# Weighted sums of cached values: four heads in four strips of output partitions, and two full transposes for eight small ones

## The reference

```python
def cross_attn(h, mem_k, mem_v, w_xq, w_xo):
    b, L, _ = h.shape
    q = (h @ w_xq).reshape(b, L, X_HEADS, X_HEAD_DIM)
    s = jnp.einsum('blhd,bmhd->bhlm', q.astype(jnp.float32), mem_k.astype(jnp.float32)) * (X_HEAD_DIM ** -0.5)
    pr = jax.nn.softmax(s, axis=-1)
    o = jnp.einsum('bhlm,bmhd->blhd', pr, mem_v.astype(jnp.float32)).reshape(b, L, D_MODEL)
    return o.astype(h.dtype) @ w_xo
...
hs, nc, ns, npool = layer(hs, state_conv[l], state_ssm[l], state_pool[l],
                          cache_mem_k[l], cache_mem_v[l], PAST_LEN, p)
```

## Time and profile before

| what | value |
|---|---|
| median of 3 runs | 1350.93 us (1350.61 to 1351.19) |
| span of the profiled execution | 1353.3 us, 2.4 us over that median; no other time is given for it |
| TensorE busy | 1289.4 us, 95% |
| VectorE busy | 743.5 us, 55% |
| ScalarE busy | 451.3 us, 33% |
| instructions | 23876 |

### The profile page before, as it was taken

How to read it: one execution, slowest core, us unless ns; L and a number is a source line. 1 busy time by engine, 2 the same in 40 slices (tenths; PEclk the granted TensorE clock), 3 DMA queues, 4 the chain that set the end, 5 groups by cost and what they waited for, 6 DMA issues and landing times.

```text
span 1353.3 us, 23876 instructions
## 1 busy us (share of the span) xinstructions
PE 1289.4 (95%) x9801; PEld 1193.5 (88%) x9801; DVE 743.5 (55%) x1484; ACT 451.3 (33%) x752; POOL 150.2 (11%) x176
## 2 busy tenths in 40 slices
PE   6999999999999898799999998899999999999996
PEld 5999988888888897689999997449999999999996
DVE  5777865656667877864344438323543443433433
ACT  4444432333332124532234323223431231322322
POOL 1000011000112957400001000001100000000000
PEclk7999989999998899999999999899999999999998
DMA  6422322222123666432233728511222222223211
GB/s 220 113 82 73 95 66 64 63 63 63 32 63 98 206 195 192 124 117 86 86 119 101 274 93 292 207 62 46 96 94 94 94 94 94 93 93 93 95 63 63
DMA packets 139214, 147.54 MB, mean 109 GB/s; under 512 B 4210, under 2 KB 132386, under 8 KB 138817
## 3 DMA queue, kind: packets, MB, share of 16 engines
q1 hardware_dynamic: 119124, 126.98, 29.3%
q10 hardware_dynamic: 18096, 8.62, 2.3%
q0 software_dynamic: 1904, 10.65, 2.2%
HBM read 130.21 MB, written 16.68 MB: 109 GB/s over the span
## 4 chain that ended last, share of the span: by engine, by line
PE 85%; DVE 8%; ACT 2%; DMA 2%; POOL 2%; issue 1%; SPq 0%; DVEq 0%; ACTq 0%
PE slot L371 67%; PE slot L1862 2%; PE aux L1624 2%; PE aux L1617 1%; PE slot L1773 1%; PE aux L1618 1%; DVE w_lo L356 1%; PE aux L1603 1%; DVE junk L1387 1%; ACT w_hi L349 1%; PE aux L1835 1%; PE slot L1853 1%; DVE sring L1199 1%; POOL win_sum L555 1%; DMA vr<-in_conv_b 1%
## 5 line engine op out<-in xcount | busy, mean ns | idle before, releaser
L356 DVE TENSOR_TENSOR w_lo<-w_raw,w_hi 128x1024 fp32r<-128x1024 f32 x186 | 234.2, 1259 | 360.9 <-ACT w_hi L349 360.8
L349 ACT ACTIVATE w_hi<-w_raw 128x1024 fp32r<-128x1024 f32 x186 | 197.0, 1059 | 571.9 <-PE slot L371 535.8
L371 PE MATMUL slot<-a_hi,w_hi 128*128 128x260 f32 x1408 | 300.8, 295 | 0.7 <-DVE a_lo L1428 0.7
L371 PE MATMUL slot<-a_hi,w_lo 128*128 128x260 f32 x1408 | 286.1, 285 | 0.0
L371 PE MATMUL slot<-a_lo,w_hi 128*128 128x260 f32 x1408 | 285.3, 285 | 0.0
L371 PEld LDWEIGHTS slot<-a_hi,w_hi 128*128 128x128 f32 x1408 | 221.5, 191 | 18.9 <-issue 15.4
L371 PEld LDWEIGHTS slot<-a_lo,w_hi 128*128 128x128 f32 x1408 | 219.9, 191 | 0.0
L371 PEld LDWEIGHTS slot<-a_hi,w_lo 128*128 128x128 f32 x1408 | 219.5, 191 | 0.0
L371 PE MATMUL slot<-b_hi,w_hi 128*128 128x260 f32 x640 | 129.0, 283 | 1.6 <-DVE gate_b L1258 1.6
L371 PE MATMUL slot<-c_hi,w_hi 128*128 128x260 f32 x640 | 129.4, 283 | 0.2 <-DVE c_lo L1340 0.2
L371 PE MATMUL slot<-b_hi,w_lo 128*128 128x260 f32 x640 | 129.0, 283 | 0.0
(11 more groups left out here) (385 smaller groups left out, 1582.4 us busy)
## 6 DMA issues: line engine op xcount, KB each, us to landing
w_raw<-in_w_in SPq DMA_DIRECT2D x32, 1024.0 KB, 5.7
w_raw<-in_w_up SPq DMA_DIRECT2D x16, 1024.0 KB, 5.3
w_raw<-in_w_down SPq DMA_DIRECT2D x16, 1024.0 KB, 5.0
sring<-in_state_ssm SPq DMA_DIRECT2D x16, 512.0 KB, 4.2
out_ssm_sample<-sring ACTq DMA_DIRECT2D x16, 512.0 KB, 3.6
w_raw<-in_w_ssd_proj SPq DMA_DIRECT2D x8, 1024.0 KB, 5.1
cache<-in_cache_mem_k SPq DMA_DIRECT2D x8, 1024.0 KB, 7.6
cache<-in_cache_mem_v SPq DMA_DIRECT2D x8, 1024.0 KB, 5.1
```

The source lines that it names most:

```text
L349: nc.scalar.activation(w_hi[:, t % 2], w_raw[:, t // 2 % 2, :, t % 2 * P:t % 2 * P + P], ACT.Copy).then_inc(hi_ready, 1)
L356: nc.vector.tensor_tensor(w_lo[:, t % 2], w_raw[:, t // 2 % 2, :, t % 2 * P:t % 2 * P + P], w_hi[:, t % 2].bitcast(F32), ALU.subtract).the ...
L371: last = nc.tensor.matmul(slot[t % 2][:, h, 0:HALF], w[:, t % 2, k, :], act[:, k, h * HALF:(h + 1) * HALF], start=(start and k == 0 and n ...
```

## The change

Each head's sums go to 32h to 32h + 7 of the output partitions, all in columns 0 to 255 of bank 1 of `slot[0]`. Each head starts its own accumulation. `o_tok` becomes 128 partitions by 256 columns and is filled by one copy instead of two; the rows between the heads' eights carry whatever the bank held. Two transposes of 128 by 128 into columns 256 to 511 of the same bank replace eight of 8 by 128, and the copies to `a_hi` and `a_lo` pick the eight used columns of each 32.

```diff
-        o_tok = at("o_tok", [NS, D], R_4 + 10240)
+        o_tok = at("o_tok", [P, XD], R_4 + 10240)
...
+        def by_head(t):
+            return t[:, :, SEQ:TT].rearrange("p (h j) b -> p h j b", j=2)
+
+        def o_turned():
+            return slot[0][:, 1, XD:2 * XD].rearrange("p (j h r) -> p h j r", j=2, h=XH)[:, :, :, 0:NS]
...
-                    nc.scalar.activation(a_hi[:, :, SEQ:TT], slot[0][:, 1, 0:64].rearrange("p (k b) -> p k b", k=KT),
-                                         ACT.Copy).then_inc(o_s_hi, 1)
+                    nc.scalar.activation(by_head(a_hi), o_turned(), ACT.Copy).then_inc(o_s_hi, 1)
...
-                    for j in range(2):
-                        nc.scalar.activation(o_tok[:, j * 512:(j + 1) * 512], slot[j][0:NS, 1, :], ACT.Copy).then_inc(o_s_row, 1)
+                    nc.scalar.activation(o_tok[:], slot[0][:, 1, 0:XD], ACT.Copy).then_inc(o_s_row, 1)
...
-                    nc.vector.tensor_tensor(a_lo[:, :, SEQ:TT], slot[0][:, 1, 0:64].rearrange("p (k b) -> p k b", k=KT),
-                                            a_hi[:, :, SEQ:TT].bitcast(F32), ALU.subtract).then_inc(o_s_lo, 1)
+                    nc.vector.tensor_tensor(by_head(a_lo), o_turned(), by_head(a_hi).bitcast(F32), ALU.subtract).then_inc(o_s_lo, 1)
...
-                    last = nc.tensor.matmul(slot[h // 2][0:NS, 1, h % 2 * XD:(h % 2 + 1) * XD], p_diag[:, m, b, h, :],
-                                            cache[n % CR][:, m, h * XD:(h + 1) * XD], start=(b == 0 and m == 0 and h % 2 == 0),
-                                            stop=(b == NS - 1 and m == 1 and h % 2 == 1), skip_group_check=True)
+                    last = nc.tensor.matmul(slot[0][32 * h:32 * h + NS, 1, 0:XD], p_diag[:, m, b, h, :],
+                                            cache[n % CR][:, m, h * XD:(h + 1) * XD], start=(b == 0 and m == 0),
+                                            stop=(b == NS - 1 and m == 1))
...
-                    pe.wait_ge(o_s_row, 2)
-                    for k in range(KT):
-                        last = nc.tensor.transpose(slot[0][:, 1, k * NS:(k + 1) * NS], o_tok[:, k * P:(k + 1) * P], ident[0:NS, 0:NS])
+                    pe.wait_ge(o_s_row, 1)
+                    for j in range(2):
+                        last = nc.tensor.transpose(slot[0][:, 1, XD + j * P:XD + (j + 1) * P], o_tok[:, j * P:(j + 1) * P], ident[:])
```

## The result

The changed kernel takes 1341.3 us (median of 20 runs, 1336.14 to 1348.24); the kernel before took 1351.1 us in the runs beside them (20 runs, 1347.16 to 1359.43). The ratio is 0.9921, 95% interval 0.9905 to 0.9937, so 8.5 to 12.8 us of 1351 were gained. The prediction said 1341.9 us.

What follows compares the result with a forecast made beforehand. The prediction took TensorE to hold the chain, with VectorE only 0.6 us behind; gains of 5.8 + 0.66 + 0.64 + 1.30 + 0.66 = 9.06 us took 1350.93 to 1341.9 us, range 1339.0 to 1350.6.

Steps and rivals of the forecast that it cites:

- all four heads at once: Rival for the weighted sums: the heads' matmuls all overlap, a group takes 0.54 us, kernel 1339.8 us; chance 0.24.
- Nothing behind the stage absorbs the gain: Gemms behind the softmax stage wait for TensorE alone, so the stage's gain reaches the end nearly whole.
- v = 1.18: Time of one four-head weighted-sum group: only neighbouring heads overlap, five slots instead of eight, 1.18 us for 1.82; chance 0.42.
- Ordinary steps 0.58: Ten softmax steps gain 0.58 us each, 5.8 in all, limited by VectorE's normalisation for any group up to 1.23 us.
- Steps behind values(h) 0.22: Steps n = 4, 8, 12, where VectorE splits the values first: gain 0.22 us each, 0.66 in all.
- Step 0: 0.64: First softmax step, at the lower clock: shorter weighted sums let scores(2) end 0.64 us earlier.
- Step 14: 1.30: Softmax step with two weighted-sum groups together: 3.55 us become 2.25, gain 1.30, bounds 0 and 2.3.
- The copy 0.66: End of the stage: one ScalarE copy of 128x256 replaces two of 8x512 ahead of step 15's exponential, gaining 0.66 us.
- the transposes nothing: End of the stage: two full transposes (0.44 us) replace eight small (0.66), hidden while TensorE waits for normalisation; no gain.
- Strip changes: Slower rival: each of 64 changes of head empties the array, 0.166 us each, 10.6 us in all, kernel 1360.9; chance 0.07.
- the clock: Slower rival: waits in each step drop TensorE to 1.2 GHz, costing some 22 us over 13 steps; chance 0.03.

Runs made afterwards that it cites:

- Head by head: Changed kernel with step 14's two halves issued one head after another instead of one half after another; stage 52.89 us against 52.97.
- the extra matmuls: Changed kernel plus two more weighted-sum calls (four instructions) in strip 3 in each group of steps 1 to 13; stage 55.15 us against 52.97.
- Two strips: Changed kernel with the heads' sums in two groups of output partitions instead of four, a 64x512 copy and four transposes; stage 54.53 us against 52.97.
- the old end: Changed kernel keeping four strips, but with four copies of 8x256 and eight small transposes at the end; stage 54.46 us against 52.97.

## Why the prediction was right, and where its working was not

The time came out 0.6 us from the forecast's 1341.9, but by way of a rival: all four heads at once (1339.8 us, 11.1 us), to which I gave 0.24. That the median fell nearer to 1341.9 is luck: the interval, 8.5 to 12.8 us, holds 9.1 and 11.1 alike, and the stage, which tells them apart, gave 11.26. By steps, from the two traces:

- **Nothing behind the stage absorbs the gain.** Right: 439 us from the first gemm to the end in both.
- **v = 1.18.** Wrong. The step that failed: "instructions start in order, head h's second waits for its first, and only then may head h+1 start". The eight start in two rounds of four and take 0.62 us in the timeline, where before's 1.89 stood for 1.82 on the chain, so v is about the rival's 0.54. Head by head and the extra matmuls show that a strip's matmuls wait for one another and not for those of another strip that stand ahead of them in the kernel.
- **Ordinary steps 0.58, whatever v is below 1.23.** Right: 2.47 us for 3.06, 0.59 each, and this is why the wrong v hardly showed. Two strips (v 0.97) left the step as it was; 1.39 in one strip lengthened it by 0.16; another order on VectorE shortened it by 0.76 with ScalarE's.
- **Steps behind values(h) 0.22.** Right: from the start of values(h) to the turn behind it 6.09 us (855.79 to 861.88) for 6.32 (864.06 to 870.38): 0.23. One line of the chain before and two of the chain after:

```profile
864.06 3.70 PE slot L1853 x8
```

```profile
855.79 3.71 PE slot L1856 x8
...
861.88 0.44 PE aux L1847 x2
```

- **Step 0: 0.64.** Mis-sized by v: to the end of scores(2), 5.15 us became 3.38 (848.72 - 845.34), 1.77. The all-at-once figure was 1.68.
- **Step 14: 1.30.** Mis-sized by v as well: turn(13) to turn(14) went from 911.03 - 906.24 = 4.79 to 895.65 - 893.18 = 2.47, so 2.32 were gained, all that the prediction's bound allowed. VectorE holds this step too now: turn(14) waits for it. (By the prediction's own order the two groups make nine slots and not ten, as head 0 of the second half and head 3 of the first lie in different strips; that would have been 1.52.) Turn(13) of before, and the turns of after:

```profile
906.24 0.44 PE L1844 MATMUL aux<-ident,prob 128*128 128x128 f32 x2
```

```profile
893.18 0.44 PE L1847 MATMUL aux<-ident,prob 128*128 128x128 f32 x2 [0.62 <-DVE prob L1423]
...
895.65 0.44 PE L1847 MATMUL aux<-ident,prob 128*128 128x128 f32 x2 [0.19 <-DVE prob L1423]
```

- **The copy 0.66, the transposes nothing.** Right: turn(14) to turn(15) takes 897.87 - 895.65 = 2.22 us for 913.92 - 911.03 = 2.89, 0.67, and the transposes, at 896.83, stand while TensorE waits for the normalisation. These lines of after answer to the earlier trace rows:

```profile
896.40 0.38 ACT L897 ACTIVATE o_tok<-slot 128x256 f32<-128x256 f32 x1
896.66 0.48 ACT L883 ACTIVATE prob<-aux,stats 128x256 f32<-128x256 f32 x1
...
896.83 0.44 PE L1894 MATMUL slot<-ident,o_tok 128*128 128x128 f32 x2 [0.75 <-ACT o_tok L897]
...
897.87 0.44 PE L1847 MATMUL aux<-ident,prob 128*128 128x128 f32 x2 [0.60 <-DVE prob L1423]
```

- **Strip changes and the clock.** Neither came. The prediction weighed a rule of the Trainium skill, page "TensorE: Matmul & The Clock Gate", "What overlaps and what doesn't": weight loads overlap running matmuls only where their row groups differ. The trace does not agree: eight loads, all on the same 128 rows, are over in 0.12 us, the last four of them while the first four matmuls run (851.24 to 851.39). In steps with 0.6 us of waiting the clock stayed at 1.00 (851 to 898). In the run with the old end it did fall, behind two us with 0.49 us of work.

What stays open: whether the engine itself takes later matmuls of a free strip ahead, or the program already stands in such an order when it reaches the engine. The traces show when matmuls start, not how they were queued.

## What to carry to other kernels

Eight matmuls with weights of 8 columns that stream different data took 0.62 us for 1.89 once their outputs lay in the four groups of 32 partitions: two rounds in place of eight, some 0.21 us apart. Count the rounds of the fullest strip, whatever the order of the calls. Before such an edit, look how far behind the next engine is: here VectorE was 0.6 us behind, and the gain of an ordinary step stopped at 0.59 of the 1.3 us that TensorE saved. More came only when that engine's order was changed too, an edit worth nothing before.

## What the runs showed of the hardware

- Full-fp32 matmuls with 8-column weights in four strips start within 0.02 us of each other, and eight instructions take 0.62 us where one strip takes 1.89. The second instructions of all four heads follow 0.22 us after the first.
- ScalarE's copies of 8x256 from four different strips follow each other at 0.40 us, while a copy of 128x256 let the next instruction start 0.26 to 0.28 us later.
- The same program ahead of the stage took from 842.8 to 851.1 us in nine profiles, with the granted clock falling in different places (400 to 500 us at 0.91 and at 1.00).
